# Up and output projection as three rounded products, with the splits shared by four engines, and an earlier feed-forward copy

## The chip, the core and the metric

The kernel runs on one core of a Trainium2 chip. The time is the device time of one execution in microseconds (us); the figure for a kernel is the median of its runs. TensorE (PE in the profile) multiplies, its weight loads are PEld; VectorE is DVE, ScalarE is ACT, GpSimd is POOL, and SyncE (SP) only issues DMAs. SBUF is the on-chip memory, PSUM the eight banks (`PB`) that TensorE writes.

## What is computed

Two transformer blocks over 256 tokens of width 1024. The change lies in the first block, between its two mixers and the expert layer, and in the feed-forward parts of the second. Cut to what matters:

```python
y_attn = dsa_attention(q, k, zv, iq, ik, ziw) @ w_up_attn[layer]          # [256,512] @ [512,1024]
y_pool = pool_mixer(zp, w_pool_grp[layer], s_pool[layer]) @ w_up_pool[layer]
g_attn, g_pool = jnp.split(jax.nn.sigmoid(zg), 2, axis=-1)
mixed = (g_attn * y_attn + g_pool * y_pool) @ w_out[layer]                # [256,1024] @ [1024,1024]
x = x + gate1 * mixed
h2 = rms_norm(x, g_norm2[layer]) * (1.0 + scale2) + shift2
x = x + gate2 * peer_ffn(h2, w_peer_q[layer], peer_subkeys[layer], peer_u[layer], peer_v[layer])
...
h = h + MACARON_WEIGHT * swiglu(rms_norm_2(h, ffn_norm[layer, 0]), ...)   # four of these, d_ff 2816
```

`peer_ffn` picks, for each token and each of 8 heads, 16 of 16384 experts and multiplies with the gathered rows of `peer_u` and `peer_v`: 256 gathers of 1 MB in the kernel.

## The kernel before

All weights stream through `ring`, four slots (`NS`) of 3072 words a partition, in units numbered by `PLAN`; unit u lies in slot u % 4. SyncE's queue loads them in one fixed order (`load`, line 428), each load waiting until the unit four back is done (`unit_done`). Each engine has one program written out by hand; semaphores tie them together. `tell` and `link` signal and then wait for the instruction's own end; `note` only signals.

The stage that the change touches runs like this. TensorE computes the last gate unit (`gates(7, 8)`, L675), transposes the attention probabilities (L740), multiplies the pooled activations with `wgrp` (L749) and the probabilities with the values (L754). VectorE and ScalarE share the evacuations. Then come four `up` units of two output chunks `dc` each: for every `dc`, eight f32 products of 256 columns (L771), attention part into the left half of bank `PB[c]`, pooled part into the right half. VectorE multiplies each half with its gate `sg` (L1450, L1451; one operand in PSUM), adds them (L1452; both in SBUF) into `mixT`, then does one step of a table for a later stage (`s5_grids`, L1259 to L1293), and after dc 3, 5 and 7 it scales arrived output units by the gate row `brow` (L1459). Two banks, so product dc+2 waits for sum dc. The output projection (L792) takes tile 0 (128 tokens) with all eight k, 16 f32 products of 512 columns, then tile 1. Behind each tile follow residual (L1494), norm, `h2_row` (L1507, L1509), transposes (L780) and copies; behind both, VectorE routes the first head of the experts (`route`), and GpSimd issues the gathers (L2404), twelve buffers deep. The small operations `s5_angles` (L1276 to L1282) and `s5_coefs` (L1299 to L1313) prepare the later stage.

The four feed-forward blocks are already computed as rounded products: an operand w is split into hi, which is w rounded to fp32r, and lo = w - hi, and hi*hi + hi*lo + lo*hi is summed. ScalarE writes `gu_hi` (`lead_gate_up`, L2208), VectorE `gu_lo` (`split_gate_up`, L1631), TensorE does 48 gate and up products of 256 columns (L874) and 12 down products of 512 (L885) per unit, 22 units a block. In the first block VectorE also builds the tables `s5_tables` (L1713 and following), one operation of 2048 columns in each of twelve units.

The lines that order this in the feed-forward part, ScalarE (2206 to 2208) and VectorE (1680 to 1684):

```python
act.wait_ge(a_done, i * NS + (a0 + j + 1))
s.copy(gu_hi[:, j % 2, :], ring[:, u % NS, 0:2 * D]).then_inc(gu_hi_done, 1)
...
activation(j)
if j + 2 < FU:
    split_gate_up(j + 2)
if f == 0:
    s5_tables(j)
```

## Time and profile before

| | us |
|---|---|
| median of 3 runs | 1990.49 (1988.64 to 1990.56) |
| the profiled execution | 1990.15 |
| its span in the profile | 1988.4 |
| TensorE busy | 1786.9 (90%) |
| VectorE busy | 1435.9 (72%) |
| ScalarE busy | 583.0 (29%) |
| GpSimd busy | 403.7 (20%) |

The page's 40 slices are 49.7 us each. The projections that are changed lie in the fourth and fifth slice, the gather in the fifth to the eighteenth, then come feed-forward block 0, the state-space mixer, blocks 1 and 2, the attention of the second layer and block 3. In the chain that ended last TensorE has 58%, VectorE 17%, DMA 16% and ScalarE 3%; the largest lines are L874 with 20%, the gathers with 15% and L885 with 9%. A matmul's end is modelled and consecutive ones overlap, so the spacing of their starts is their price, not the duration in a row. An f32 matmul appears as two records.

### The profile page before, as it was taken

The numbers are of one execution on the slowest core, as the hardware profiler recorded it, in microseconds if no ns is written. First come the engines' busy times: TensorE is split into PE (matmuls) and PEld (weight loads), VectorE is DVE, ScalarE is ACT, GpSimd is POOL, SyncE is SP. The second block draws the span as 40 slices with busy tenths as digits, with TensorE's granted clock in tenths as the row PEclk, the third lists the DMA queues.
The fourth block names the chain that finished last, engine by engine and source line by source line (L and its number), as shares of the span: only waits on it lengthen the run. The fifth ranks groups of instructions, "written<-read, shape, count | busy, mean of one in ns | idle before, by whom it ended". The sixth has DMA issues, their size and how long they took to land.

```text
span 1988.4 us, 24322 instructions
## 1 busy us (share of the span) xinstructions
PE 1786.9 (90%) x9244; PEld 1335.5 (67%) x9244; DVE 1435.9 (72%) x2699; ACT 583.0 (29%) x754; POOL 403.7 (20%) x368
## 2 busy tenths in 40 slices
PE   6999888777777877789999898999999999989999
PEld 4787553333333333338889777899989997779998
DVE  7887588888888888767777697565566555867555
ACT  1232110011001100005444310354554544456442
POOL 0010144444544445420000188000000000000000
PEclk8999999889988899999999999999999999999999
DMA  9853499999999999984444421535554554534553
GB/s 394 336 187 106 150 419 421 421 422 421 422 421 421 419 418 419 406 343 191 174 185 169 148 86 64 198 141 190 190 191 159 190 190 141 185 112 160 186 190 116
DMA packets 63851, 502.09 MB, mean 253 GB/s; under 512 B 7200, under 2 KB 7456, under 8 KB 11296
## 3 DMA queue, kind: packets, MB, share of 16 engines
q0 software_dynamic: 37008, 268.98, 32.7%
q1 hardware_dynamic: 25776, 229.40, 31.4%
q10 hardware_dynamic: 992, 2.74, 0.3%
q8 instruction: 43, 0.70, 0.1%
q14 instruction: 32, 0.26, 0.0%
HBM read 500.04 MB, written 1.05 MB: 252 GB/s over the span
## 4 chain that ended last, share of the span: by engine, by line
PE 58%; DVE 17%; DMA 16%; issue 4%; ACT 3%; POOL 1%; SPq 0%; DVEq 0%; ACTq 0%; POOLq 0%
PE PB L874 20%; DMA arena<-in_uv,eidx 11%; PE PB L885 9%; PE PB L856 8%; DMA ring<-in_uv,eidx 4%; PE PB L675 3%; DVE arena L1580 3%; PE PB L557 2%; PE PB L1014 2%; PE PB L604 2%; ACT gu_hi L2208 1%; PE PB L839 1%; PE PB L792 1%; PE PB L661 1%; PE PB L771 1%
## 5 line engine op out<-in xcount | busy, mean ns | idle before, releaser
L856 PE MATMUL PB<-arena 128*128 128x512 f32 x604 | 312.4, 676 | 94.2 <-DVE arena L1591 94.2
L874 PE MATMUL PB<-h_hi,gu_hi 128*128 128x256 f32 x1344 | 378.0, 281 | 5.0 <-DVE gu_lo L1631 4.9
L874 PE MATMUL PB<-h_hi,gu_lo 128*128 128x256 f32 x1344 | 377.0, 280 | 0.0
L874 PE MATMUL PB<-h_lo,gu_hi 128*128 128x256 f32 x1344 | 375.8, 280 | 0.0
L856 PEld LDWEIGHTS PB<-arena 128*128 128x128 f32 x604 | 127.1, 216 | 279.0 <-issue 151.9
L1631 DVE TENSOR_TENSOR gu_lo<-ring,gu_hi 128x2048 fp32r<-128x2048 f32 x85 | 194.9, 2293 | 158.4 <-ACT gu_hi L2208 158.1
L2404 POOL DMA_INDIRECT arena<-in_uv,eidx x193 | 220.0, 1140 | 338.0 <-PE PB L856 220.5
L1580 DVE CUSTOM_DVE_ANT_0 arena<-arena,XN 128x1024 f32<-128x1024 f32 x187 | 223.2, 1222 | 67.6 <-DMA arena<-in_uv,eidx 67.3
L874 PEld LDWEIGHTS PB<-h_hi,gu_hi 128*128 128x128 f32 x1344 | 254.1, 189 | 12.7 <-DVE gu_lo L1631 10.0
L874 PEld LDWEIGHTS PB<-h_lo,gu_hi 128*128 128x128 f32 x1344 | 252.0, 188 | 2.7
L874 PEld LDWEIGHTS PB<-h_hi,gu_lo 128*128 128x128 f32 x1344 | 252.7, 188 | 0.0
L2208 ACT CAST gu_hi<-ring 128x2048 fp32r<-128x2048 f32 x84 | 160.4, 1910 | 152.0 <-DVE a_lo L1653 151.8
L2186 ACT ACTIVATE gl<-dots 128x4 f32<-128x4 f32 x62 | 12.7, 205 | 438.2 <-DVE dots L1580 438.1
L885 PE MATMUL PB<-dn_hi,a_hi 128*128 128x512 f32 x352 | 138.8, 394 | 0.1
L885 PE MATMUL PB<-dn_lo,a_hi 128*128 128x512 f32 x352 | 138.2, 393 | 0.0
L885 PE MATMUL PB<-dn_hi,a_lo 128*128 128x512 f32 x352 | 137.2, 390 | 0.0
L856 PE MATMUL PB<-ring,act_gs 128*128 128x512 f32 x168 | 82.4, 636 | 34.9 <-DVE act_gs L1591 34.9
L1636 DVE TENSOR_TENSOR dn_lo<-ring,dn_hi 128x1024 fp32r<-128x1024 f32 x88 | 107.0, 1216 | 0.0
L1641 DVE TENSOR_TENSOR act_gs<-PB,XN 128x256 f32<-128x256 f32 x88 | 37.3, 424 | 94.6 <-PE PB L874 92.9
L2216 ACT ACTIVATE act_gs<-act_gs 128x256 f32<-128x256 f32 x88 | 36.9, 419 | 233.5 <-DVE act_gs L1641 233.5
L2404 POOL DMA_INDIRECT ring<-in_uv,eidx x63 | 80.3, 1274 | 84.7 <-PE PB L856 75.0
L2212 ACT CAST dn_hi<-ring 128x1024 fp32r<-128x1024 f32 x88 | 92.3, 1049 | 5.9 <-PE PB L885 5.6
(407 smaller groups left out, 2920.6 us busy)
## 6 DMA issues: line engine op xcount, KB each, us to landing
ring<-in_ffn SPq DMA_DIRECT2D x88, 1536.0 KB, 6.4
arena<-in_ada SPq DMA_DIRECT2D x24, 768.0 KB, 9.2
ring<-in_qkv SPq DMA_DIRECT2D x12, 1024.0 KB, 4.8
ring<-in_zg SPq DMA_DIRECT2D x8, 1024.0 KB, 5.2
ring<-in_s5b SPq DMA_DIRECT2D x8, 1024.0 KB, 4.8
ring<-in_ada SPq DMA_DIRECT2D x4, 1536.0 KB, 13.7
ring<-in_up SPq DMA_DIRECT2D x4, 1024.0 KB, 4.8
ring<-in_wo SPq DMA_DIRECT2D x4, 1024.0 KB, 4.9
```

The lines of the kernel that those rows point to most:

```text
L557: mm = pe.matmul(PB[c][:, 0:T], lhsT=w_chunk(u, c, k), rhs=src[:, k, :], start=(k == 0), stop=(k == DC - 1))
L604: mm = pe.matmul(PB[2 + 2 * t + n][:, :], lhsT=h[:, k, t * P:(t + 1) * P], rhs=w[:, w_part % 2, o:o + 512], start=(k == 0 and m == 0), sto ...
L675: mm = pe.matmul(PB[c][:, 0:T], lhsT=w_chunk(u, c, k), rhs=hT[:, k, :], start=(k == 0), stop=(k == DC - 1))
L856: mm = pe.matmul(PB[2 + 2 * t + h][:, :], lhsT=diag(n), rhs=uv[n % UVB][:, 1, h * 512:(h + 1) * 512], start=False, stop=False, skip_group_ ...
L874: mm = pe.matmul(PB[j % 2][:, b * T:(b + 1) * T], lhsT=w[:, j % 2, o:o + P], rhs=h[:, k, :], start=(k == 0 and m == 0), stop=(k == DC - 1 ...
L885: mm = pe.matmul(PB[2 + 2 * t + h][:, :], lhsT=x[:, j % 2, t * P:(t + 1) * P], rhs=w[:, j % 2, h * 512:(h + 1) * 512], start=False, stop=( ...
L1580: v.tensor_tensor_reduce(out=u[:, 0, :], in0=u[:, 0, :], in1=XN[:, t, :], scale=1.0, scalar=0.0, op0=ALU.mult, op1=ALU.add, accum_out=dots ...
L1631: v.tensor_tensor(gu_lo[:, j % 2, :], ring[:, (u0 + j) % NS, 0:2 * D], gu_hi[:, j % 2, :].bitcast(F32), ALU.subtract).then_inc(gu_lo_done, 1)
L1636: v.tensor_tensor(dn_lo[:, j % 2, :], ring[:, (u0 + j) % NS, 2 * D:3 * D], dn_hi[:, j % 2, :].bitcast(F32), ALU.subtract).then_inc(dn_lo_d ...
L2208: s.copy(gu_hi[:, j % 2, :], ring[:, u % NS, 0:2 * D]).then_inc(gu_hi_done, 1)
L2212: s.copy(dn_hi[:, j % 2, :], ring[:, (u0 + j) % NS, 2 * D:3 * D]).then_inc(dn_hi_done, 1)
L2404: g.indirect_dma_start(uv[j].rearrange("p a d -> p (a d)"), None, a["uv"], bass.IndirectOffsetOnAxis(ap=eidx[:, t, h * PK + i:h * PK + i + 1],
```

## The change

Up and output projection become rounded products, like the feed-forward blocks. There are now three products for one. What is split, and by whom:

- up units: hi by ScalarE (`split_up`), lo by GpSimd for units 0, 2, 3 (two instructions of 1024 columns each) and by VectorE for unit 1.
- output units: scaled by VectorE (0, 1) or GpSimd (2, 3), hi by ScalarE, lo by GpSimd (0, 1) or VectorE (2, 3).
- activations: ScalarE writes `yp_hi`, `ya_hi`, `mix_hi`, VectorE `y_lo` and, in each dc, `mix_lo`.

Since up units 2 and 3 are fully copied out of their slots, SyncE loads output units 2 and 3 into them as soon as GpSimd has split them, in the order 2, 0, 3, 1, and the sub-keys `skd` behind them (before: ScalarE's queue, much earlier). The pooled product is ahead of the wait for the probabilities' copies. `s5_angles` moves between the two softmax halves, `s5_coefs` behind the first routing unit. In the feed-forward blocks ScalarE's copy of unit j+2 waits for the products of unit j (`gu_done`) instead of VectorE's last operation of unit j (`a_done`), and the table comes before the split.

```diff
-            load("wo", 4)
+            for i in (2, 0, 3, 1):
+                u = UNIT[("wo", i)]
+                if i < 2:
+                    sp.wait_ge(unit_done, u - NS + 1)
+                else:
+                    sp.wait_ge(w_lo_pool, i)
+                sp.dma_start(ring[:, u % NS, 0:PLAN[u][2]], a["wo"][i]).then_inc(w_here[u % NS], 16)
+            sp.dma_start(skd[:, :, :], a["skd"]).then_inc(sk_here, 16)
...
+            pe.wait_ge(tz_done, 22)
+            for g in range(4):
+                pe.matmul(PB[g // 2][:, (g % 2) * T:(g % 2 + 1) * T], lhsT=wgrp[:, g, :], rhs=pw0[:, g, 0:T],
+                          start=True, stop=True).then_inc(pg_full, 1)
             pe.wait_ge(pt_act, 3)
             pe.wait_ge(pt_dve, 3)
...
-                    for b, src in enumerate((yat, ypT)):
+                    for b, src in ((1, yp_hi), (0, ya_hi)):
+                        if dc == 0:
+                            pe.wait_ge(y_lo_done, 4 if b else 6)
                         for k in range(4):
-                            mm = pe.matmul(PB[c][:, b * T:(b + 1) * T], lhsT=w_chunk(u, c, 4 * b + k),
-                                           rhs=src[:, k, :], start=(k == 0), stop=(k == 3))
+                            o = (4 * b + k) * P
+                            hi, lo = up_hi[i][:, c * D + o:c * D + o + P], up_lo(i, c)[:, o:o + P]
+                            for m, (w, y) in enumerate(((hi, src[:, k, :]), (hi, y_lo[:, b, k, :]), (lo, src[:, k, :]))):
+                                mm = pe.matmul(PB[c][:, b * T:(b + 1) * T], lhsT=w, rhs=y,
+                                               start=(k == 0 and m == 0), stop=(k == 3 and m == 2))
...
                     if t == 0:
-                        pe.wait_ge(wo_scaled, i + 1)
+                        if i < 2:
+                            pe.wait_ge(w_lo_pool, 6 + i)
+                        else:
+                            pe.wait_ge(w_lo_dve, 2 + i)
...
             softmax_out(0, 1, L1, T)
-            s5_angles()
+            split_up(1)
...
-                tell(v.tensor_tensor(mixT[:, dc, :], tmp[:, 0, 0:T], tmp[:, 1, 0:T], ALU.add), mixT_done)
+                tell(v.tensor_tensor(tmp[:, c, T:2 * T], tmp[:, 0, 0:T], tmp[:, 1, 0:T], ALU.add), mix_sum)
+                if dc:
+                    mix_low(dc - 1)
                 s5_grids(dc)
...
+                if dc in (3, 4):
+                    scale_wo(dc - 3)
+            mix_low(DC - 1)
+            split_wo(2)
+            split_wo(3)
...
                 for step in range(4):
                     route(k, step)
+                if k == 0:
+                    s5_coefs()
...
+                    if f == 0:
+                        s5_tables(j)
                     if j + 2 < FU:
                         split_gate_up(j + 2)
-                    if f == 0:
-                        s5_tables(j)
...
+            for dc in range(DC):
+                act.wait_ge(mix_sum, dc + 1)
+                s.copy(mix_hi[:, dc, :], tmp[:, dc % 2, T:2 * T]).then_inc(mix_hi_done, 1)
+                if dc == 3:
+                    act.wait_ge(w_lo_dve, 2)
+                    split_wo(0)
+                if dc == 4:
+                    act.wait_ge(w_lo_dve, 3)
+                    act.wait_ge(unit_done, UNIT[("up", 1)] + 1)
+                    split_wo(1)
...
-                    act.wait_ge(a_done, i * NS + (a0 + j + 1))
+                    if a0 + j > 1:
+                        act.wait_ge(gu_done, i * NS + (a0 + j - 1))
...
+            split_up(2)
+            split_up(3)
+            for i in (2, 3):
+                u = UNIT[("wo", i)]
+                pool.wait_ge(w_here[u % NS], 16 * (u // NS + 1))
+                pool.wait_ge(brow_act, 2)
+                wv = ring[:, u % NS, 0:2 * D].rearrange("p (a b) -> p a b", b=D)
+                tell(g.tensor_tensor(wv, wv, brow[:, 0, :].unsqueeze(1).broadcast_to([P, 2, D]), ALU.mult), w_lo_pool)
+            for i in (0, 1):
+                pool.wait_ge(w_hi, 4 + i + 1)
+                tell(g.tensor_tensor(wo_lo(i), ring[:, UNIT[("wo", i)] % NS, 0:2 * D], wo_hi[i][:, :].bitcast(F32),
+                                     ALU.subtract), w_lo_pool)
```

GpSimd's program between its start and the first gather, before (L2381 to L2388 are the window sums of the pooled activations):

```order
16 L2381 TENSOR_TENSOR arena<-arena 128x257
17 L2386 TENSOR_TENSOR arena<-arena 128x256 x4
18 L2388 TENSOR_TENSOR arena<-arena 128x4x256
19 L2404 DMA arena<-in_uv,eidx 128x2048 x7
```

and after (L2489 is `split_up`, L2519 the scaling of output units 2 and 3, L2522 the split of 0 and 1):

```order
17 L2503 TENSOR_TENSOR arena<-arena 128x257
18 L2508 TENSOR_TENSOR arena<-arena 128x256 x4
19 L2510 TENSOR_TENSOR arena<-arena 128x4x256
20 L2489 TENSOR_TENSOR ring_r<-ring,up_hi_63 128x1024 x2
21 L2489 TENSOR_TENSOR ring_r<-ring,up_hi_64 128x1024 x2
22 L2519 TENSOR_TENSOR ring<-ring,arena 128x2048 x2
23 L2522 TENSOR_TENSOR ring_r<-ring,wo_hi_65 128x2048
24 L2522 TENSOR_TENSOR ring_r<-ring,wo_hi_66 128x2048
25 L2539 DMA arena<-in_uv,eidx 128x2048 x7
```

Eight instructions of 1024 or 2048 columns now stand between the window sums and the first gather.

VectorE in the up projection, dc 3 to the first product of dc 4, before (L1450 to L1452 products and sum, L1267 and L1269 a grid step, L1459 the scaling of output unit 0):

```order
135 L1450 TENSOR_TENSOR arena<-PB,arena 128x256
136 L1451 TENSOR_TENSOR arena<-PB,arena 128x256
137 L1452 TENSOR_TENSOR arena<-arena 128x256
138 L1267 TENSOR_TENSOR base_hi<-s5p,iota 128x256
139 L1269 TENSOR_SCALAR base_hi<-base_hi 128x256
140 L1459 TENSOR_TENSOR ring<-ring,arena 128x2048
141 L1450 TENSOR_TENSOR arena<-PB,arena 128x256
```

and after (the same lines are now L1520 to L1522, L1304, L1306 and L1500; L1511 is `mix_low`):

```order
138 L1520 TENSOR_TENSOR arena<-PB,arena 128x256
139 L1521 TENSOR_TENSOR arena<-PB,arena 128x256
140 L1522 TENSOR_TENSOR arena<-arena 128x256
141 L1511 TENSOR_TENSOR mix_lo<-arena,mix_hi 128x256
142 L1304 TENSOR_TENSOR base_hi<-s5p,iota 128x256
143 L1306 TENSOR_SCALAR base_hi<-base_hi 128x256
144 L1500 TENSOR_TENSOR ring<-ring,arena 128x2048
145 L1520 TENSOR_TENSOR arena<-PB,arena 128x256
```

Each dc has one more operation with both inputs in SBUF.

VectorE in the first feed-forward block, a unit with a table, before (L1653 ends the activation, L1631 is the split, L1713 the table, L1641 starts the next unit):

```order
1341 L1653 TENSOR_TENSOR a_lo<-act_a,a_hi 128x256
1342 L1631 TENSOR_TENSOR gu_lo<-ring,gu_hi 128x2048
1343 L1713 TENSOR_TENSOR arena<-base_hi,base_lo 128x2048
1344 L1641 TENSOR_TENSOR act_gs<-PB,XN 128x256
```

and after:

```order
1350 L1724 TENSOR_TENSOR a_lo<-act_a,a_hi 128x256
1351 L1784 TENSOR_TENSOR arena<-base_hi,base_lo 128x2048
1352 L1702 TENSOR_TENSOR gu_lo<-ring,gu_hi 128x2048
1353 L1712 TENSOR_TENSOR act_gs<-PB,XN 128x256
```

The table and the split have changed places.

## Rows read from the trace of the kernel before

**Rows 1.** TensorE timeline: start, duration (us), line, operation, operands, count, [idle, releaser].
```profile
158.33 2.79 PE L754 MATMUL PB<-arena 128*64 128x512 f32 x12
162.19 27.86 PE L771 MATMUL PB<-arena,ring 128*128 128x256 f32 x128 [1.06 <-DVE arena L1440]
191.60 20.87 PE L792 MATMUL PB<-ring,arena 128*128 128x512 f32 x48 [1.55 <-DVE arena L1452]
...
213.33 7.03 PE L792 MATMUL PB<-ring,arena 128*128 128x512 f32 x16
```

**Rows 2.** VectorE timeline: a mask ahead of it, the up projection, behind it.
```profile
132.09 2.87 DVE L1424 TENSOR_TENSOR arena<-PB,arena 128x512 f32<-128x512 f32 x4 [5.23 <-PE PB L712]
...
165.99 0.42 DVE L1450 TENSOR_TENSOR arena<-PB,arena 128x256 f32<-128x256 f32 x1 [4.06 <-PE PB L771]
...
191.12 0.42 DVE L1452 TENSOR_TENSOR arena<-arena 128x256 f32<-128x256 f32 x1
...
205.71 1.42 DVE L1494 TENSOR_TENSOR X<-PB,X 128x512 f32<-128x512 f32 x2 [4.98 <-PE PB L792]
...
211.12 1.22 DVE L1509 TENSOR_TENSOR XN<-XN,arena 128x1024 f32<-128x1024 f32 x1
```

**Rows 3.** Window table: length, busy us (instructions) of PE PEld DVE ACT POOL, clock, DMA.
```profile
164.00:190.00 26.00, 26.00 (x121) 22.60 (x119) 19.76 (x40) 0.00 (x0) 0.00 (x0) 1.00 0.35 122
```

**Rows 4.** TensorE timeline: rounded products, 512 columns, then 256 at either clock.
```profile
926.64 0.40 PE L885 MATMUL PB<-dn_hi,a_hi 128*128 128x512 f32 x1
926.87 0.39 PE L885 MATMUL PB<-dn_lo,a_hi 128*128 128x512 f32 x1
...
1108.59 0.41 PE L573 MATMUL PB<-h_hi,gu_hi 128*128 128x256 f32 x1
1108.81 0.41 PE L573 MATMUL PB<-h_lo,gu_hi 128*128 128x256 f32 x1
...
1112.26 0.28 PE L573 MATMUL PB<-h_hi,gu_lo 128*128 128x256 f32 x1
1112.38 0.28 PE L573 MATMUL PB<-h_hi,gu_hi 128*128 128x256 f32 x1
```

**Rows 5.** GpSimd timeline, two stretches.
```profile
150.08 2.40 POOL L2388 TENSOR_TENSOR arena<-arena 128x1024 f32<-128x1024 f32 x1
...
1227.90 1.26 POOL L2450 TENSOR_TENSOR arena<-arena 128x512 f32<-128x512 f32 x1
1229.12 1.71 POOL L2451 TENSOR_TENSOR arena<-arena 128x512 f32<-128x512 f32 x1
```

**Rows 6.** VectorE timeline, the same stretches.
```profile
150.30 2.22 DVE L1259 TENSOR_SCALAR s5p<-s5p 128x32 f32<-128x32 f32 x1
...
1221.52 0.69 DVE L1788 TENSOR_TENSOR PB<-PB,arena 128x512 f32<-128x512 f32 x1
...
1227.91 1.79 DVE L1831 TENSOR_TENSOR arena<-arena 128x512 f32<-128x512 f32 x1
1229.63 1.74 DVE L1832 TENSOR_TENSOR arena<-arena 128x512 f32<-128x512 f32 x1
```

**Rows 7.** VectorE timeline in the first feed-forward block.
```profile
933.67 2.29 DVE L1631 TENSOR_TENSOR gu_lo<-ring,gu_hi 128x2048 fp32r<-128x2048 f32 x1 [1.97 <-ACT gu_hi L2208]
935.88 2.28 DVE L1715 TENSOR_TENSOR arena<-base_hi,base_lo 128x2048 f32<-128x2048 f32 x1
```

**Rows 8.** Source view of the gate and up products: first block, third block.
```profile
L874 PE MATMUL PB<-h_hi,gu_hi x336: 279/280/390, 912.5 to 1093.1; 128*128 128x256 f32 x168
...
L874 PE MATMUL PB<-h_hi,gu_hi x336: 278/280/382, 1490.2 to 1663.9; 128*128 128x256 f32 x168
```

**Rows 9.** ScalarE timeline: a rounding copy, and the first gelu of the gather.
```profile
1341.54 1.91 ACT L2208 CAST gu_hi<-ring 128x2048 fp32r<-128x2048 f32 x1 [1.92 <-DVE a_lo L1653]
...
266.97 0.20 ACT L2186 ACTIVATE gl<-dots 128x4 f32<-128x4 f32 x1
```

**Rows 10.** Window table of the gather, columns as in Rows 3.
```profile
300.00:400.00 100.00, 81.46 (x168) 33.58 (x166) 84.01 (x226) 8.90 (x17) 48.31 (x43) 0.91 1.01 421
```

More of the change, by code:

```diff
@@ L191, in build @@
         sq = part(5632, TT, 12, HD)
-        vn = part(7168, TT, HD)
+        vn = part(28488, TT, HD)
         iw = part(7296, TT, IH)
@@ L787, in _ @@
                     if t == 0:
-                        pe.wait_ge(wo_scaled, i + 1)
+                        if i < 2:
+                            pe.wait_ge(w_lo_pool, 6 + i)
+                        else:
+                            pe.wait_ge(w_lo_dve, 2 + i)
                     for k in (2 * i, 2 * i + 1):
-                        for n in range(2):
-                            o = (k - 2 * i) * D + n * 512
-                            mm = pe.matmul(PB[2 + 2 * t + n][:, :], lhsT=mixT[:, k, t * P:(t + 1) * P],
-                                           rhs=ring[:, u % NS, o:o + 512], start=(k == 0), stop=(k == DC - 1))
+                        if t == 0:
+                            pe.wait_ge(mixT_done, k + 1)
+                        for m, (x, w) in enumerate(((mix_hi, wo_hi[i]), (mix_hi, wo_lo(i)), (mix_lo, wo_hi[i]))):
+                            for n in range(2):
+                                o = (k - 2 * i) * D + n * 512
+                                mm = pe.matmul(PB[2 + 2 * t + n][:, :], lhsT=x[:, k, t * P:(t + 1) * P],
+                                               rhs=w[:, o:o + 512], start=(k == 0 and m == 0),
+                                               stop=(k == DC - 1 and m == 2))
                     if t:
@@ L1427, in _, with split_up @@
                 softmax_in(0, t, (L, L1)[t], S, range(4), HD ** -0.5, masks)
+                if t == 0:
+                    s5_angles()
+            def split_up(i):
+                dve.wait_ge(w_hi, i + 1)
+                u = UNIT[("up", i)]
+                note(v.tensor_tensor(ring_r[:, u % NS, 0:2 * D], ring[:, u % NS, 0:2 * D], up_hi[i][:, :].bitcast(F32),
+                                     ALU.subtract), w_lo_dve)
             softmax_out(0, 0, L, P)
@@ L2096, in gate_sigmoids, with split_up @@
                     tell(s.activation(sg[:, c, :], PB[c % 2][:, 0:T], ACT.Sigmoid), tz_done)
+            def split_up(i):
+                u = UNIT[("up", i)]
+                act.wait_ge(w_here[u % NS], 16 * (u // NS + 1))
+                s.copy(up_hi[i][:, :], ring[:, u % NS, 0:2 * D]).then_inc(w_hi, 1)
             relus(0)
@@ L2126, in _, with split_wo @@
                 tell(s.copy(PT[:, k, 0, :], PB[PT_BANK[k]][:, :]), pt_act)
-            for g in (0, 2):
-                act.wait_ge(pg_full, g + 1)
-                tell(s.activation(ypT[:, g, :], PB[2 + g][:, 0:T], ACT.Copy, scale=col("s_pool")[:, g:g + 1]), pg_act)
+            for g in range(4):
+                act.wait_ge(pg_full, g // 2 * 2 + 2)
+                s.activation(yp_hi[:, g, :], PB[g // 2][:, (g % 2) * T:(g % 2 + 1) * T], ACT.Copy,
+                             scale=col("s_pool")[:, g:g + 1]).then_inc(y_hi_done, 1)
+            for t in range(TT):
+                act.wait_ge(av_full, t + 1)
+                s.copy(ya_hi[:, :, t * P:(t + 1) * P],
+                       PB[6 + t][:, :].rearrange("p (j q) -> p j q", j=4)).then_inc(y_hi_done, 1)
+            act.wait_ge(mixp_ready, 1)
+            split_up(3)
+            def split_wo(i):
+                s.copy(wo_hi[i][:, :], ring[:, UNIT[("wo", i)] % NS, 0:2 * D]).then_inc(w_hi, 1)
+            for dc in range(DC):
[8 more added lines that the diff above has]
+                    split_wo(1)
+            act.wait_ge(w_lo_pool, 4)
+            act.wait_ge(unit_done, UNIT[("up", 3)] + 1)
+            split_wo(2)
+            act.wait_ge(w_lo_pool, 5)
+            split_wo(3)
             def keep_h2(t):
@@ L2373, in _, with split_up @@
             tell(g.memset(pT[:, :, 0:16], 0.0), ident_ready)
+            def split_up(i):
+                pool.wait_ge(w_hi, i + 1)
+                for c in range(2):
+                    cs = slice(c * D, (c + 1) * D)
+                    ins = g.tensor_tensor(up_lo(i, c), ring[:, UNIT[("up", i)] % NS, cs], up_hi[i][:, cs].bitcast(F32),
+                                          ALU.subtract)
+                    if c == 0:
+                        link(ins)
+                    else:
+                        tell(ins, w_lo_pool)
+            split_up(0)
             pool.wait_ge(p_ready, 1)
```

91 lines of the change are left out of this document (57 added, 34 removed).

## The prediction

> **What bounds the kernel now.** I read the chain of waits first, then the timelines of TensorE and VectorE over the stage that is changed (about 146 to 230 us), then the window table, and last the first feed-forward block. Four stretches matter. (1) The up and output projections are bound by TensorE: 128 records of 256 columns in 27.9 us, then 64 of 512 columns in 27.9 us [rows 1]; VectorE follows each up product (first one at 165.99, last sum at 191.12 to 191.54) and holds up little [rows 2]. (2) The gather from about 245 to 880 us is bound by DMA: the window shown is one of six at a DMA share of 1.01 and about 420 GB/s, a seventh has 1.00 [rows 10]. Its first request stands behind the h2 rows of both tiles on VectorE (the first tile's at 211.12 [rows 2], the second's comes after the last output product), so what the projections gain or lose moves the whole gather, one for one. (3) The first feed-forward block is paced by VectorE, the other three by TensorE [rows 8]. (4) The rest is untouched.
>
> **Products.** An f32 product shows as two records; those of 256 columns start 27.86/128 = 0.215 us apart, so one costs 0.43; one of 512 columns costs 2 x 27.9/64 = 0.87 [rows 1]. A rounded product is one record: 0.12 apart at 256 columns, 0.23 at 512 [rows 4]. Three of them make 0.35 and 0.69. TensorE saves 64 x 0.077 = 4.9 us in the up and 32 x 0.18 = 5.7 us in the output projection, 10.6 together. That is the ceiling; the walk below says how much is collected.
>
> **Start of the up projection.** The pooled product moves ahead of the evacuations of the transposed probabilities, and the products on it begin while the attention part is still being rounded. Against that, ScalarE puts a copy of a whole up unit (1.91 us, the like of [rows 9]) ahead of its three evacuations. By the walk the attention product ends at 160.0 instead of 161.1 [rows 1], the first up product reaches VectorE at 163.5 instead of 165.99 [rows 2]: 2.5 us earlier.
>
> **VectorE with GpSimd left aside.** Before, from first product to last sum it takes 25.5 us, of which it is idle only in part: in 164 to 190 it is busy 19.8 us in 40 instructions [rows 3], and with some 0.03 us between instructions and the work up to 191.54 its own sequence comes to 22.4 us (eight times three operations of 0.42, grid steps, two scalings of 2.29, the duration that 128x2048 has in [rows 7]). The change adds seven subtractions of 0.42 + 0.03 (mix_low) before the last sum, keeps two scalings: 22.4 + 3.2 = 25.6. TensorE would need only 8 x 2.83 = 22.6. So VectorE becomes the bound and the last sum comes at 163.5 + 25.5 = 189.0, 2.5 earlier and no more. Behind it the second half of the output units needs two subtractions (0.9, overlapping) and a ScalarE copy (1.9) and a VectorE split (2.3): ready 193.8. Before, TensorE went on 0.06 us after the sum [rows 1, 2]. The first four of eight k of tile 0 are done by then; the last four take 24 x 0.23 = 5.5, to 199.3; tile 1 takes 11.0 and 0.9 of transposes, with 1.6 of waiting, since from tile 0's residual to its h2 row takes 205.71 to 212.34 [rows 2]. End 212.9, against 213.33 + 7.03 = 220.4 [rows 1]: **-7.4**.
>
> **GpSimd and VectorE.** This is the term that decides. The change gives GpSimd ten instructions of 1024 or 2048 columns with two inputs in SBUF, the last six of them beside the up projection; one of 1024 takes 2.40, one of 512 1.26 [rows 5], so by that slope one of 2048 takes 4.7 (an estimate). The trace shows what happens when both engines read two SBUF operands: VectorE's L1831, 512 columns, takes 1.79 where its neighbour with one PSUM operand takes 0.69 [rows 6]; it ends 0.54 us after GpSimd's L2450 ends at 1229.16, and then GpSimd's L2451 takes 1.71 instead of 1.26 [rows 5], and VectorE's L1832 again 1.74. A VectorE tensor_scalar of 32 columns lasts 2.22, to the end of GpSimd's 2.40 [rows 6, 5]. So one waits for the whole of the other's instruction, and they take turns. The products L1450 and L1451 read PSUM and are free of it; the sum, mix_low and the grid steps are not.
> Walk it from 163.5: GpSimd runs the second half of unit 3 (2.4), the scalings of output units 2 and 3 (4.7 each) back to back from 165.2, and each time VectorE has had its turn the next one goes. VectorE waits 0.7 (first sum), 2.1 and 4.4 (two grid steps of dc 0), 4.1 (sum of dc 1). Then GpSimd has nothing until ScalarE has rounded output unit 0, and its two splits of 4.7 fall on the grid steps of dc 4 and 5: 4.4 and 4.4. Together 20.1; some 0.3 falls where VectorE had waited anyway: **+19.8**. The exclusion alone bounds it from below: VectorE's 25.6 and GpSimd's 22.8 us from 163.5 on, less the 16 free products of 0.45 that may lie beside (7.2), end at 204.7 at the earliest; TensorE needs GpSimd's last split for six of the eight k of tile 0 (8.3), and 13.5 for tile 1: 226.5, so some 13.6 are lost even with the best of orders, if what the trace shows holds. From above: all 23.5.
> [...]
>
> **Clock.** TensorE then stands idle for 7 us before output unit 2. After such idling the trace shows products at 0.215 instead of 0.12 apart [rows 4], the 1.2 GHz level, for some 3 us: I take **+1.5**, between 0 and 3. Earlier idling lies under VectorE.
>
> **What costs nothing.** s5_angles (eleven small operations, about 2.4 us) goes into a VectorE idle time of 5.23 before the second mask [rows 2]. s5_coefs (3.6) goes behind the first routing unit: its first dots come 3.6 later, at 265.5, still ahead of the gelu at 266.97 [rows 9], which waits for ScalarE; without that cover it would cost 3.6. The sub-keys' load moves to SyncE's queue behind the last output unit; its user comes 40 us later. The early up loads are as before; output units load sooner, but SyncE now waits for GpSimd's splits, which only the turns above delay. The change adds no wait that a queued DMA of the gather feels.
>
> **Feed-forward.** In the first block VectorE splits the next weights 1.97 us after ScalarE was let go, and then builds a table (2.28) [rows 7]; the gate and up products of 21 units spread over 1093.1 - 912.5 = 180.6 us, against 1663.9 - 1490.2 = 173.7 in the third block [rows 8]. With the copy released by gate_up and the table ahead of the split, VectorE's cycle falls from 9.2 to about 7.3 us, under TensorE's 8.4: **-6.9**, with 0 and -7.5 as ends. The other blocks have TensorE without idling there: 0.
>
> **Sum.** -7.4 + 19.8 + 1.5 - 6.9 = +7.0 on the profiled execution's 1990.15, which lies 0.3 under the median of 1990.49: **1997**.
>
> **Rivals.** (a) GpSimd does not hold VectorE up, because its splits land in idle time or don't take the turn: -7.4 - 6.9 gives 1976, faster. For it: before, only a few instructions meet; against: each contested pair in the trace waits. It decides as soon as the six waits together are under 13.1 us. (b) The turns cost half, 10 us, because VectorE gets several operations into each gap: 1987. Against it: L1832 lost its turn though it followed at once [rows 6], and the bound of 13.6 above. (c) The block gains nothing, because something else paces VectorE: 2004. Against it: the third block runs with the same products at 8.4 a unit. (d) GpSimd's rounded output, which no row of the trace has, runs 1.5 times as long: 7 us each, the walk gives +10.7 more: 2008.
>
> **How the numbers follow.** Forecast 0.56, (a) 0.15, (b) 0.13, (c) 0.09, (d) 0.07. What a measurement here can tell from no change is 0.2%, 4 us: the same is 1986.5 to 1994.5. Faster: (a) and most of (b), 0.23. Same: the rest of (b) and the low edge of the forecast, 0.11. Slower: 0.66. The range 1980 to 2008 leaves out (a) and the far side of (d).
>
> **What would show it.** The profile after: VectorE's sum and grid steps in 163 to 205 us with single durations of 2 to 5 us instead of 0.3 to 0.7, ending with GpSimd's instructions; last sum near 209; TensorE idle before output unit 2 with a clock of about 0.5 behind it; GpSimd at 2.4 and 4.7; the first gather request some 14 us later than before; the first block's products over 174 us. If VectorE's sums there take 0.42 throughout, the forecast is wrong and (a) is right.

## The result, and the profile after

The changed kernel takes 1993.67 us (median of 9 runs, 1990.05 to 1998.37) against 1990.49 of before beside it (9 runs, 1984.78 to 1990.86): a ratio of 1.0023, 95% interval 1.0013 to 1.0032, so 2.6 to 6.4 us slower, 4.6 at the centre. The forecast was 1997, slower. The interval leaves out no change; but the prediction had called a time of 1986.5 to 1994.5 "the same", and the median lies inside that band, while before times the ratio, 1995.1, lies just outside: the slowdown is shown, and it is small. The profiled execution has a span of 1993.2 against 1988.4.

Before the changed stage the profile after already runs 1.0 us late, in code that is the same in both. All comparisons below take off what two traces differ by ahead of the stage; where I call a time "from the anchor", it is counted from one VectorE instruction (a product read of 128x256 at 123.60 before, 124.59 after).

VectorE of the kernel after, from the first up product to the second tile's residual (columns: start, duration, engine, line, operation, output and inputs with shapes, count; in brackets the idle time in front and what ended it). It answers to [rows 2] and [rows 3]:

```profile
164.07 0.42 DVE L1520 TENSOR_TENSOR arena<-PB,arena 128x256 f32<-128x256 f32 x1 [1.76 <-PE PB L802]
...
164.99 1.22 DVE L1522 TENSOR_TENSOR arena<-arena 128x256 f32<-128x256 f32 x1
166.24 2.78 DVE L1304 TENSOR_TENSOR base_lo<-s5p,iota 128x512 f32<-128x512 f32 x1
169.06 4.62 DVE L1306 TENSOR_SCALAR base_lo<-base_lo 128x512 f32<-128x512 f32 x1
173.71 0.42 DVE L1520 TENSOR_TENSOR arena<-PB,arena 128x256 f32<-128x256 f32 x1
...
175.88 5.06 DVE L1297 TENSOR_TENSOR base_lo<-base_lo,arena 128x512 f32<-128x512 f32 x1
...
191.08 6.55 DVE L1500 TENSOR_TENSOR ring<-ring,arena 128x2048 f32<-128x2048 f32 x1
...
200.96 3.75 DVE L1522 TENSOR_TENSOR arena<-arena 128x256 f32<-128x256 f32 x1
...
207.08 0.43 DVE L1522 TENSOR_TENSOR arena<-arena 128x256 f32<-128x256 f32 x1
...
217.96 1.42 DVE L1563 TENSOR_TENSOR X<-PB,X 128x512 f32<-128x512 f32 x2 [3.68 <-PE PB L828]
...
231.39 1.42 DVE L1563 TENSOR_TENSOR X<-PB,X 128x512 f32<-128x512 f32 x2 [4.83 <-PE PB L828]
```

GpSimd in the same stretch, the timeline of after:

```profile
163.53 4.95 POOL L2489 TENSOR_TENSOR ring_r<-ring,up_hi 128x1024 fp32r<-128x1024 f32 x2 [2.28 <-ACT up_hi L2172]
168.56 4.84 POOL L2519 TENSOR_TENSOR ring<-ring,arena 128x2048 f32<-128x2048 f32 x1
175.83 4.56 POOL L2519 TENSOR_TENSOR ring<-ring,arena 128x2048 f32<-128x2048 f32 x1 [2.44 <-issue]
190.75 4.73 POOL L2522 TENSOR_TENSOR ring_r<-ring,wo_hi 128x2048 fp32r<-128x2048 f32 x1 [10.35 <-ACT wo_hi L2221]
199.70 4.72 POOL L2522 TENSOR_TENSOR ring_r<-ring,wo_hi 128x2048 fp32r<-128x2048 f32 x1 [4.22 <-ACT wo_hi L2221]
```

Read the two together. L1522 at 200.96 ends at 204.71; GpSimd's last split ends at 204.42. L1297 at 175.88 ends at 180.94, GpSimd's second scaling at 180.39. Each time the long VectorE instruction ends within its own uncontested duration of the end of GpSimd's. The six waits are 0.8, 2.1, 4.2, 4.4, 4.3 and 3.3: 19.1 us. Each contested L1522 stands behind products from PSUM (L1520, L1521) that keep their 0.42, although GpSimd is at work beside them too. The 4.2 are on L1306, which has only one SBUF operand: a tensor_scalar is held up as well, as the prediction's walk had it.

TensorE after, its idle times of over 1 us in the up and output projection:

```profile
175.11 0.58 PE L802 MATMUL PB<-yp_hi,up_hi 128*128 128x256 f32 x1 [5.40 <-DVE arena L1522]
182.46 0.35 PE L802 MATMUL PB<-yp_hi,up_hi 128*128 128x256 f32 x1 [1.86 <-DVE arena L1522]
190.06 0.35 PE L802 MATMUL PB<-yp_hi,up_hi 128*128 128x256 f32 x1 [1.62 <-DVE arena L1522]
198.93 0.58 PE L802 MATMUL PB<-yp_hi,up_hi 128*128 128x256 f32 x1 [5.81 <-DVE arena L1522]
...
212.13 0.74 PE L828 MATMUL PB<-wo_hi,mix_hi 128*128 128x512 f32 x2 [1.93 <-DVE ring_r L1505]
224.66 1.09 PE L810 MATMUL PB<-ident,XN 128*128 128x128 f32 x8 [1.22 <-DVE XN L1578]
```

Before, the same stage had TensorE at work nearly without a gap [rows 1]; now each of its long waits ends with a VectorE instruction. The first gather request stands at 252.84 against 241.74: 10.1 later from the anchor. The feed-forward block 0 then takes 1098.6 - 924.9 = 173.7 us instead of the 180.6 of [rows 8] (view of one source line: count, duration min/median/max in ns, first and last start):

```profile
L911 PE MATMUL PB<-h_hi,gu_hi x336: 279/280/384, 924.9 to 1098.6; 128*128 128x256 f32 x168
```

So the profile's 4.8 us are 1.0 ahead of the stage, 10.1 in it, 1.3 over the gather, -6.9 in block 0 and -0.7 in all that follows.

### The profile page after: what moved, and what is told of

Read it like the earlier page. It is cut to its first block, busy times and chain, and to the rows that moved or that the text cites. A ratio compares the mean times of both kernels' runs of the same rounds, so it can differ in the third digit from the quotient of the medians.

```text
span 1993.2 us, 24604 instructions
## 1 busy us (share of the span) xinstructions
PE 1780.7 (89%) x9340; PEld 1345.3 (67%) x9340; DVE 1456.3 (73%) x2710; ACT 603.1 (30%) x774; POOL 439.0 (22%) x378
## 4 chain that ended last, share of the span: by engine, by line
PE 61%; DVE 17%; DMA 16%; issue 2%; POOL 2%; ACT 2%; SPq 0%; DVEq 0%; ACTq 0%; POOLq 0%
PE PB L911 24%; PE PB L922 11%; DMA arena<-in_uv,eidx 11%; PE PB L893 7%; DMA ring<-in_uv,eidx 5%; PE PB L702 3%; DVE arena L1649 2%; PE PB L584 2%; PE PB L1051 2%; PE PB L631 2%; PE PB L688 1%; PE PB L999 1%; DVE gu_lo L1234 1%; PE PB L937 1%; POOL arena L2539 1%
## 5 line engine op out<-in xcount | busy, mean ns | idle before, releaser
L893 PE MATMUL PB<-arena 128*128 128x512 f32 x604 | 307.0, 667 | 90.6 <-DVE arena L1660 90.6
L893 PE MATMUL PB<-ring,act_gs 128*128 128x512 f32 x168 | 88.9, 679 | 38.7 <-DVE act_gs L1660 38.7
L893 PEld LDWEIGHTS PB<-ring,act_gs 128*128 128x128 f32 x168 | 34.7, 215 | 91.7 <-DVE act_gs L1660 53.2
## 6 DMA issues: line engine op xcount, KB each, us to landing
ring<-in_ada SPq DMA_DIRECT2D x4, 1536.0 KB, 13.9
```

Source lines behind the costliest of these rows:

```text
L893: mm = pe.matmul(PB[2 + 2 * t + h][:, :], lhsT=diag(n), rhs=uv[n % UVB][:, 1, h * 512:(h + 1) * 512], start=False, stop=False, skip_group_ ...
```

## The experiments

A time is the median; where a few microseconds matter the ratio to before stands with it.

**The two parts apart.** First the feed-forward edits alone, on the kernel before (e1), and the projections alone, on the kernel after (e2).

```diff
-                    act.wait_ge(a_done, i * NS + (a0 + j + 1))
+                    if a0 + j > 1:
+                        act.wait_ge(gu_done, i * NS + (a0 + j - 1))
...
-                    if j + 2 < FU:
-                        split_gate_up(j + 2)
                     if f == 0:
                         s5_tables(j)
+                    if j + 2 < FU:
+                        split_gate_up(j + 2)
```

> The kernel before with the two edits of the feed-forward block alone: ScalarE's copy of the next gate and up weights waits for the gate and up products of two units ago, and in block 0 VectorE builds the table ahead of the next split. My theory (VectorE's cycle paced block 0, and the projections' loss begins behind it): block 0's products over 173.7 us instead of 180.6, the kernel 6.9 us shorter than before, 1983.6. The rival that this gain is not there without the later start of the gather (something else paces the block): 1990, no change.

> The changed kernel with the two edits of the feed-forward block undone, so the projections' change alone. My theory (the parts add up): 4.6 + 6.9 = 11.5 us over before, 2002.0; the first gather request 11 us later than before, all the difference there already. The rival that both parts share something (the block's start): between 1994 and 1998.

Measured: e1 1981.94 us, ratio 0.9963 (0.9951 to 0.9976), 7.4 us under before. e2 2000.33, 1.0049 (1.0037 to 1.0061), 9.8 over. The source view of the gate and up products, e1 and then e2:

```profile
L874 PE MATMUL PB<-h_hi,gu_hi x364: 280/280/390, 910.7 to 1299.8; 128*128 128x256 f32 x182
```

```profile
L911 PE MATMUL PB<-h_hi,gu_hi x336: 278/280/390, 923.3 to 1104.0; 128*128 128x256 f32 x168
```

e2 has 180.7 us in block 0, as before had (the row of e1 runs on into block 1; its block 0 ends at 1084.3, 173.6 us). From the anchor e2's gather comes 10.0 later than before's, e1's 0.3 sooner. The parts add up within the noise: 9.8 - 7.4 = 2.4, where each of the two is known to about 2.5, against 4.6 (2.6 to 6.4) measured together. The gain belongs to the feed-forward edits alone, and the projections lose some 10; the rival of 1994 to 1998 for e2 is out.

**Is it GpSimd?** e3 keeps GpSimd's instructions and cuts them to 64 columns.

```diff
-                    ins = g.tensor_tensor(up_lo(i, c), ring[:, UNIT[("up", i)] % NS, cs], up_hi[i][:, cs].bitcast(F32),
+                    W = 64 if i > 1 else D
+                    cs = slice(c * D, c * D + W)
+                    ins = g.tensor_tensor(up_lo(i, c)[:, 0:W], ring[:, UNIT[("up", i)] % NS, cs], up_hi[i][:, cs].bitcast(F32),
...
-                wv = ring[:, u % NS, 0:2 * D].rearrange("p (a b) -> p a b", b=D)
+                wv = ring[:, u % NS, 0:64]
...
-                tell(g.tensor_tensor(wo_lo(i), ring[:, UNIT[("wo", i)] % NS, 0:2 * D], wo_hi[i][:, :].bitcast(F32),
+                tell(g.tensor_tensor(wo_lo(i)[:, 0:64], ring[:, UNIT[("wo", i)] % NS, 0:64], wo_hi[i][:, 0:64].bitcast(F32),
```

> The changed kernel with GpSimd's instructions beside the up projection kept in number, order and semaphores, but cut to 64 columns each: the low parts of up units 2 and 3, the scaling of output units 2 and 3, the low parts of output units 0 and 1; TensorE reads the high part in place of each low part (so part of the scaling and of the low parts is left out, at the same count of products). Turns theory: VectorE's sums and grid steps fall to their own 0.3 to 0.7 us, the six waits (19.1 us by the trace of after) go, last sum near 189, and the kernel is 18 to 20 us shorter than after: 1974 to 1976. The rival that VectorE's own longer sequence and its hand-offs with ScalarE took the time, GpSimd's being only work beside it: less than 5 us shorter than after, 1989 to 1994. The rival that the turns are half of it: 1983 to 1985.

Measured: 1974.12 us, 0.9926 (0.9911 to 0.9941): 14.7 under before, 19.3 under after by the two ratios, 19.6 by the medians. VectorE's last sums in e3:

```profile
180.37 0.42 DVE L1522 TENSOR_TENSOR arena<-arena 128x256 f32<-128x256 f32 x1
...
182.87 0.42 DVE L1522 TENSOR_TENSOR arena<-arena 128x256 f32<-128x256 f32 x1
...
185.68 0.42 DVE L1522 TENSOR_TENSOR arena<-arena 128x256 f32<-128x256 f32 x1
```

The last sum is 27.5 us behind the first up product (158.15), in after it is 46.2 behind (160.88): 18.7 of the 19.1 us of waits are gone. The theory holds, and the rival that VectorE's own sequence took the time is out. The -7.4 for the rest of the projections' change is borne out too: e3 is 7.8 under e1 by the medians, and from the anchor its second residual comes 8.9 sooner than e1's, which is the 7.4 and the 1.5 by which start and sequence turned out shorter (below).

**Which property of GpSimd's instructions?** e4 has GpSimd fill the same columns with a constant, twice, in place of each instruction with two operands.

```diff
+                        link(g.memset(up_lo(i, c).bitcast(F32), 0.0))
+                        ins = g.memset(up_lo(i, c).bitcast(F32), 0.0)
```

> The changed kernel with the same GpSimd instructions beside the up projection over their full columns, but as constant fills (they write SBUF and read nothing), two in a row in place of each; TensorE reads the high part in place of GpSimd's low parts (scaling of output units 2 and 3 and these low parts are left out). My theory (one engine waits for the other only where both read two SBUF operands): VectorE's sums and grid steps stay at 0.3 to 0.7 us although GpSimd is busy beside them, and the time is that of the run with 64 columns, 1973 to 1976. The rival that any GpSimd instruction holds VectorE up for its length: sums and grid steps of several us, 1985 to 1994.

Measured: 1976.92 us, 0.9929 (0.9913 to 0.9945), a little over the forecast, between e3 and after and by its interval e3's; the rival of 1985 to 1994 is out. The timelines of GpSimd and VectorE in e4:

```profile
185.21 1.81 POOL L2527 MEMSET ring_r<- 128x2048 f32 x1 [1.02 <-ACT wo_hi L2221]
187.08 1.81 POOL L2528 MEMSET ring_r<- 128x2048 f32 x1
```

```profile
186.49 0.42 DVE L1522 TENSOR_TENSOR arena<-arena 128x256 f32<-128x256 f32 x1
186.94 0.42 DVE L1511 TENSOR_TENSOR mix_lo<-arena,mix_hi 128x256 fp32r<-128x256 f32 x1
187.29 1.64 DVE L1327 COPY s5p<-s5p 128x32 f32<-128x32 f32 x1
188.96 0.18 DVE L1328 TENSOR_SCALAR s5p<-s5p 128x32 f32<-128x32 f32 x1
```

The sum and mix_low run at 0.42 while GpSimd fills 2048 columns beside them. A mere fill is no hindrance to an instruction with two SBUF operands. But the copy of 32 columns, one operand, behind them takes 1.64 instead of 0.18: it ends at 188.93, the fill at 188.89. Two tensor_scalar instructions wait as well (L1296 takes 1.14 instead of 0.42, L1306 0.58 instead of 0.43); together with the copy this is 2.3 us, of the 2.8 by which e4's first gather request comes later from the anchor than e3's. So my theory was too narrow: in this trace what GpSimd reads is in the way of VectorE's two-operand instructions, and what it writes in the way of its copies and tensor_scalars. The Trainium skill ("SBUF — State Buffer", "Who interferes with whom") says just this: a two-operand instruction contends with reads alone, while a copy or tensor_scalar in a two-port mode takes the whole shared pair. The fills are shorter than the instructions that they replace (two of 1.81 against 4.7), so e4 shows the kind of conflict by its rows more than by its time.

**Does the length of one instruction matter?** e6 cuts each into pieces of 256 columns (the cut shows the low parts of output units 0 and 1; the others are cut in the same way, which makes 40 pieces beside the up projection in place of six instructions, and 56 in place of all ten).

```diff
+                for q in range(8):
+                    qs = slice(q * 256, (q + 1) * 256)
+                    tell(g.tensor_tensor(wo_lo(i)[:, qs], ring[:, UNIT[("wo", i)] % NS, qs], wo_hi[i][:, qs].bitcast(F32),
+                                         ALU.subtract), pool_link if q < 7 else w_lo_pool)
```

> The changed kernel with each GpSimd instruction of the stage cut into pieces of 256 columns (about 0.6 us each by the 4.8 us of 2048; 40 pieces in place of 8 instructions), nothing left out. Turns theory (one waits for the other's current instruction, then has its turn): no VectorE wait over 0.7 us; some 28 two-operand VectorE instructions meet pieces at 0.3 to 0.6 each, 8 to 12 us in place of 19.1, GpSimd's last pieces later; 4 to 9 us under after, 1985 to 1990. The rival that the lock passes back only when GpSimd's queue of ready work is empty, or that only the sum of both engines' work counts: within 3 us of after, 1991 to 1996.

Measured: 1987.09 us, 0.9987 (0.9977 to 0.9996), 7.2 us under after by the ratios. VectorE, GpSimd and then TensorE in e6:

```profile
176.54 0.42 DVE L1520 TENSOR_TENSOR arena<-PB,arena 128x256 f32<-128x256 f32 x1
177.00 0.42 DVE L1521 TENSOR_TENSOR arena<-PB,arena 128x256 f32<-128x256 f32 x1
177.46 0.72 DVE L1522 TENSOR_TENSOR arena<-arena 128x256 f32<-128x256 f32 x1
178.22 0.84 DVE L1511 TENSOR_TENSOR mix_lo<-arena,mix_hi 128x256 fp32r<-128x256 f32 x1
178.98 0.95 DVE L1304 TENSOR_TENSOR base_hi<-s5p,iota 128x256 f32<-128x256 f32 x1
```

```profile
170.58 16.04 POOL L2524 TENSOR_TENSOR ring<-ring,arena 128x256 f32<-128x256 f32 x16
186.70 15.33 POOL L2529 TENSOR_TENSOR ring_r<-ring,wo_hi 128x256 fp32r<-128x256 f32 x16
```

```profile
202.08 1.22 PE L828 MATMUL PB<-wo_hi,mix_hi 128*128 128x512 f32 x2 [3.68 <-POOL ring_r L2529]
203.10 1.05 PE L828 MATMUL PB<-ring_r,mix_hi 128*128 128x512 f32 x2
```

Both engines now wait at nearly every step, each for one instruction of the other: no VectorE wait over 0.55, but 30 of them, 13.0 us in all where the six had 19.1; and GpSimd's 16 pieces take 16.0 us, 1.0 each, where whole ones took 9.4 in two. Part of that is the cutting itself: the first eight pieces (156.32 to 162.74), beside which all of VectorE's instructions read PSUM, take 0.80 each, against the 0.6 that I expected. The last sum ends 6.0 us sooner behind the first up product than in after, the second residual and the first gather request only 4.4 from the anchor. The rest goes on TensorE, in a way that I had not forecast: it waits 3.68 us for GpSimd's last piece, which now ends at 202.03, and its products then come 0.85 instead of 0.46 apart until 208.17 (granted clock 0.51 in 202.0 to 208.2), which is 2.7 us more. The kernel's 7.2 are more than the 4.4 of the trace; the intervals of the two ratios reach that far. The turns go back and forth by instruction, as forecast, the rival of no gain is out, and two thirds of the waiting remain.

**A remedy that takes work away.** In e5 the output weights are not scaled; the gate row is multiplied onto the product in the residual.

```diff
-                if dc in (3, 4):
-                    scale_wo(dc - 3)
...
-                for n in range(2):
-                    xs = X[:, t, n * 512:(n + 1) * 512]
-                    tell(v.tensor_tensor(xs, PB[2 + 2 * t + n][:, :], xs, ALU.add), x_done)
+                if t == 0:
+                    dve.wait_ge(brow_act, 2)
+                residual_row(0, t, XN[:, t, :])
```

GpSimd's two scalings go as well, and with the scalings ScalarE's waits for them.

> The changed kernel, its feed-forward edits included, with the output weights not scaled at all: the gate row is multiplied onto the output product when the residual is taken (as the later residuals do), so two VectorE scalings of 2.3 us and two GpSimd ones of 4.7 go, and each residual takes two more VectorE operations per tile. Turns theory: GpSimd meets VectorE at four instructions instead of six, the stage ends some 10 us sooner than in after, the kernel at 1983 to 1984, under before. The rival that ScalarE's rounding of the output units or the last up products set the start of the output projection anyway: the two added operations behind each tile show instead, 1 to 3 us over after, 1995 to 1997.

Measured: 1987.30 us, 0.9984 (0.9976 to 0.9993): 6.4 under after by the medians, not 10; the rival of 1995 to 1997 is out. Four waits are left, 0.8, 2.1, 4.4 and 4.3, and the first residual does come 10.8 us sooner than in after, from the anchor. Where 4.4 of these went, the timelines of e5 show, VectorE's residuals and TensorE between them, with the window table behind it (columns as in [rows 3]):

```profile
206.95 0.69 DVE L1525 TENSOR_TENSOR XN<-PB,arena 128x512 f32<-128x512 f32 x1 [3.67 <-PE PB L828]
...
223.22 0.69 DVE L1525 TENSOR_TENSOR XN<-PB,arena 128x512 f32<-128x512 f32 x1 [5.36 <-PE PB L828]
```

```profile
215.10 1.97 PE L810 MATMUL PB<-ident,XN 128*128 128x128 f32 x8 [2.68 <-DVE XN L1568]
```

```profile
215.10:218.00 2.90, 2.90 (x11) 2.71 (x12) 0.69 (x1) 0.59 (x1) 0.00 (x0) 0.50 0.47 198
```

The two tiles are 16.3 us apart; in after they are 13.4. TensorE stands in the middle of the second tile's products, at the transposes of the first tile's h2 rows, and these come later by what the longer residual takes: 2.68 us of idle time instead of 1.22. That is half of the 2.9. The other half is the clock: behind this idle time the granted clock is 0.50 until 218.0, and the eight transposes take 1.97 us instead of 1.09. In e7 below, the same wait, 2.67 us, is followed by a granted clock of 1.00 and the tiles are 14.9 apart. I had counted the residual's 1.5 us once, behind the last tile. e8 and e10 try this reading from two sides: e8 has the row in the residual on top of e1, with f32 products and no GpSimd in it; e10 is e5 with the transposes one output unit later.

```diff
-                        if i == 1:
+                        if i == 2:
                             h2_transposes(0)
```

> The kernel before with the feed-forward edits, and the gate row in the residual in place of the four scalings of the output weights on VectorE (f32 products kept, no rounding). My theory (before, the up projection is paced by TensorE, so that VectorE's four scalings of 2.3 us are hidden, and only the residual's added operations show): 0 to 2 us over the feed-forward edits alone, 1982 to 1984. The rival that the scalings held TensorE up: 3 to 9 us under it, 1973 to 1979, and then most of what the row in the residual gains would be had without rounded products.

> The run with the gate row in the residual (1987.3) with one move: the transposes of the first tile's h2 rows behind the third instead of the second output unit of tile 1. My theory (the residual's two more operations cost twice, once in the second tile itself and once because TensorE waits for the first tile's h2 rows between the output units): the second residual 13.4 instead of 16.3 us behind the first, 1984.5. The rival that the added operations cost once only, and the move merely shifts the wait to the second tile's transposes: 1987.

Measured: e8 1987.36 us, 0.9988 (0.9977 to 0.9998), 5.0 over e1 by the ratios. That is more than the 0 to 2 that I expected of it; the rival, a gain, is out: before the change VectorE's scalings were hidden. In its trace the tiles are 16.2 apart and in e1 14.8 (TensorE idles 1.37 at the transposes, in e1 no idle time is shown there), which with the last residual's 1.5 makes 2.9; from the anchor the gather is 3.3 later. What is left to 5.0 lies within the intervals of the two ratios, and no row shows it. e10 1983.36, 0.9958 (0.9944 to 0.9972): 3.9 under e5 by the medians. Its two residuals start at 206.44 and 218.55, 12.1 apart, even less than the 13.4 that I expected, because after had a wait there too (the 1.22 at 224.66 above). Of the 4.2 us that the tiles are closer together than in e5, 2.7 are the wait and 1.4 the slow clock behind it. That both sit at the transposes is shown; the rival of 1987 is out.

**A kernel that beats both.** e7 is e5 with two changes: VectorE also takes the low parts of output units 0 and 1 from GpSimd, and the first grid step goes ahead of the sums. Against e5:

```diff
+            s5_grids(0)
             for dc in range(DC):
...
-                s5_grids(dc)
+                if dc:
+                    s5_grids(dc)
+                if dc == 5:
+                    split_wo(0)
             mix_low(DC - 1)
+            split_wo(1)
             split_wo(2)
```

> The run with the gate row in the residual (1987.3), and besides: VectorE takes the low parts of output units 0 and 1 from GpSimd (2.3 us each, unit 0 behind sum 5, unit 1 behind the last sum), and the first grid step goes ahead of the up products' sums. GpSimd then meets VectorE only in up unit 3's low part. Turns theory: waits of at most 0.9 us at two sums; last sum near 188 to 190, first gather request some 9 us sooner than before plus 1 for the longer residual, the kernel at 1973 to 1977, under both kernels and under the feed-forward edits alone (1981.9). The rival that VectorE's own sequence grows as much as the waits shrink (2 x 2.3 against 8.5): 1982 to 1985.

Measured: 1979.70 us, 0.9953 (0.9940 to 0.9966), 3 to 7 over what I expected, under the rival's 1982 to 1985, and hardly under e1. Of the waits two short ones are left (0.7 and 0.5, at the first two sums), and the last sum is 26.0 us behind the first up product. But TensorE in e7:

```profile
189.99 0.81 PE L825 MATMUL PB<-wo_hi,mix_hi 128*128 128x512 f32 x2 [3.62 <-DVE ring_r L1494]
190.60 1.06 PE L825 MATMUL PB<-ring_r,mix_hi 128*128 128x512 f32 x2
191.45 1.06 PE L825 MATMUL PB<-wo_hi,mix_lo 128*128 128x512 f32 x2
...
196.77 0.63 PE L825 MATMUL PB<-wo_hi,mix_lo 128*128 128x512 f32 x2
```

It had run through output unit 0 before the last sum, then stood 3.6 us for unit 1's low part, and after this idle time its first products come 0.85 apart in place of 0.46, the 1.2 GHz level: up to 193.97 that makes 1.6 us more than the same products take in e9. With the 2.67 at the transposes, of which some was expected, these are the places where the gain was lost. e9 makes three moves against them at once; only the one at the transposes was also tried alone (e10). Against e7:

```diff
-                if dc == 5:
-                    split_wo(0)
-            mix_low(DC - 1)
-            split_wo(1)
+                if dc in (5, 6):
+                    split_wo(dc - 5)
+            mix_low(DC - 1)
...
             for dc in range(DC):
+                if dc == DC - 1:
+                    act.wait_ge(unit_done, UNIT[("up", 3)] + 1)
+                    split_wo(2)
                 act.wait_ge(mix_sum, dc + 1)
...
-            act.wait_ge(unit_done, UNIT[("up", 3)] + 1)
-            split_wo(2)
             split_wo(3)
...
-                        if i == 1:
+                        if i == 2:
                             h2_transposes(0)
```

> The run with the row in the residual and all output splits on VectorE (1979.7), with three moves, taken from its trace: VectorE takes the low part of output unit 1 before the last sum (TensorE stood 3.62 us for it, and then 2 us more at half clock); ScalarE rounds output unit 2 before the last mix copy; the transposes of the first tile's h2 rows go behind the third instead of the second output unit of tile 1 (TensorE stood 2.67 there for the longer residual). My theory: TensorE's part behind the last sum is the path, so the first residual comes about 2.5 us sooner after the up products' start and the second another 2.7; 1974 to 1976. The rival that the last sum, which comes 2.3 later, sets the end: no gain but the 2.7, 1977 to 1978.

Measured: 1972.54 us, 0.9910 (0.9895 to 0.9925): 17.7 under before by the medians, 21.1 under after, 9.4 under the feed-forward edits alone, and 1.5 under what I expected. From the anchor its first gather request comes 4.9 us sooner than e7's and 9.2 sooner than before's; with the 6.9 of block 0 that makes 16 of the 17.7. VectorE's residuals and TensorE's idle times in the first tile's output projection, e9:

```profile
198.46 0.69 DVE L1526 TENSOR_TENSOR XN<-PB,arena 128x512 f32<-128x512 f32 x1 [3.67 <-PE PB L825]
...
210.56 0.69 DVE L1526 TENSOR_TENSOR XN<-PB,arena 128x512 f32<-128x512 f32 x1 [2.06 <-PE PB L825]
```

```profile
188.29 0.73 PE L825 MATMUL PB<-wo_hi,mix_hi 128*128 128x512 f32 x2 [1.47 <-DVE ring_r L1494]
...
192.64 0.74 PE L825 MATMUL PB<-wo_hi,mix_hi 128*128 128x512 f32 x2 [1.31 <-DVE ring_r L1494]
```

The last sum comes later than in e7 (28.2 us behind the first up product), yet the first residual is 2.1 sooner from there and the second another 2.8: what counts is TensorE's path, the rival that the last sum sets the end is out, and after two waits of under 1.5 us TensorE ran at full speed.

## Why the prediction was right, point by point

The direction and the mechanism held: slower, because GpSimd and VectorE hold each other up in the up projection, and less so than it could be, because of the feed-forward block.

- **Start of the up projection: held.** Forecast 163.5 for the first product on VectorE, and 163.1 came (164.07 less the 1.0 ahead of the stage).
- **VectorE's own sequence: 1.1 too long.** 25.5 us from first product to last sum; 207.51 - 164.07 less 19.1 of waits is 24.4. Most of the difference is `mix_low`: the next instruction starts 0.34 us behind its start, not 0.45, seven times.
- **The turns: held, wait by wait.** Forecast 0.7, 2.1, 4.4, 4.1, 4.4, 4.4 = 20.1; measured 0.8, 2.1, 4.2, 4.4, 4.3, 3.3 = 19.1. The last three sit on other instructions than I wrote (the second grid operation of dc 1, the scaling behind dc 4, the sum of dc 6). One reason is in the rows: GpSimd's second scaling starts 2.4 us after the first has ended, not back to back. The sixth is 1.1 shorter since VectorE was busy with two PSUM reads when GpSimd began. e3 takes them all away and gains 19.3; the bound of 13.6 held, and rivals (a) and (b) are out.
- **GpSimd's rounded output (rival d): out.** 4.73 and 4.72 us for 2048 columns, against the estimate of 4.7; the f32 scalings take 4.84 and 4.56. The Trainium skill ("GPSIMD Engine Reference", section 3.1) has 4497 ns for an f32 tensor_tensor of 2048 columns; the trace is 0.1 to 0.3 above.
- **The clock: wrong place and size.** +1.5 forecast for a slow stretch before output unit 2. TensorE was slow after its idle times of 5.40 and 5.81, in the up products, where VectorE was busy without a gap and hid it; before output unit 2 it stood only 1.93 us, not 7, since the last up products kept it until 204.22 (2.4 of that by the slow clock) and output units 0 and 1 until 210.20; the products behind the 1.93 ran at full speed. So 0. In e5, e6 and e7, where VectorE was no longer the bound at that point, such a slow stretch did show, at 1.4, 2.7 and 1.6 us: the term was real, and that after paid nothing for it was the luck of where it fell.
- **What was to cost nothing: held.** TensorE reached the end of the stage with no new wait on s5_angles, s5_coefs or the sub-keys; from the second residual to the first gather request it is 21.45 after and 21.27 before. s5_coefs lies behind that request; the first gelu comes 25.45 us behind it after and 25.23 before, so it was covered as forecast.
- **Feed-forward: held.** 173.7 us as forecast, by e1 worth 7.4 us on the kernel (4.8 to 9.8); rival (c) is out.
- **The sum.** +7.0 forecast, +4.8 in the profile. The stage gave 9.9 to 10.1 instead of 13.9 (0.4 from the start, 1.1 the sequence, about 0.8 the turns, 1.5 the clock). Against this stand 1.0 ahead of the stage and 1.3 over the gather, less 0.7 in what follows block 0. None of these has a cause in the change that the runs show: from gather request to block 0 the profiles of e1, e2 and e3 need 671.2, 670.9 and 670.1 us, those of before and after 670.8 and 672.1; and in the first 124 us, in unchanged code, they differ by up to 3 us. So the stage was forecast 3.8 us too dear, by four terms of which only the clock had its mechanism in the wrong place, and 1.6 us of drift in unchanged code brought the total nearer by luck: 2.2 us of error in the profile, 3 by the medians.

## What to carry to other kernels

Work given to an idle GpSimd is not free beside a VectorE that works at its limit: where GpSimd reads two SBUF operands, take each VectorE instruction that can meet it as done one after the other, if it reads two SBUF operands or is a tensor_scalar within SBUF, and add up both engines. Instructions with an operand in PSUM were free of it. Cutting GpSimd's instructions shorter made the waits even and a third smaller (13.0 us left of 19.1), and the pieces cost more each; a work of 2.3 us on VectorE was better than a meeting of 4.3 with GpSimd (e7 against e5). When an operation is moved or made longer, look once more at every point where another engine waits in the middle of its stretch (here the transposes): a delay of 1.5 us came back there a second time, and in e5 the slow clock behind it cost as much again.

## What the runs showed of the hardware that I had not expected

- A constant fill by GpSimd (128x2048, 1.81 us) leaves VectorE's two-operand instructions at 0.42, but holds up a copy of 32 columns (1.64 instead of 0.18) until it ends.
- With pieces of 256 columns on GpSimd, both engines take turns over most of 38 us: 1.0 us for a piece, which takes 0.80 where nothing meets it and by the whole instructions (4.7 for 2048) would take 0.6.
- TensorE's granted clock was at the 1.2 GHz level (about 0.5) behind idle times of 5.40 and 5.81 us in after (products 0.21 to 0.22 apart instead of 0.12), 3.68 in e6, 3.62 in e7 and 2.68 in e5, and at full speed behind 2.73 in e4, 2.67 in e7, 1.93 in after and 1.47 and 1.31 in e9. So the length of the idle time alone does not decide near 2.7 us; what else does, no run shows.
- The same unchanged code ahead of the stage took between 121.6 and 124.8 us in the profiled executions of these kernels. A difference of 3 us between two profiles is therefore none until it is counted from a common instruction behind that stretch.
